# Attention scores computed already turned, with row maxima from a first rough product, and more of the elementwise work on GpSimd

## What is computed

```python
s = jnp.einsum('bqhd,bkhd->bhqk', qn, k_nope) + jnp.einsum('bqhd,bkd->bhqk', qr, k_rope)
pr = jax.nn.softmax(s.astype(jnp.float32) * scale, axis=-1).astype(v.dtype)
return jnp.einsum('bhqk,bkhd->bqhd', pr, v)
```

## Time and profile before

| | |
|---|---|
| median of 3 runs | 1148.6 us (1147.55 to 1149.5) |
| the profiled execution | 1144.88 us, its span 1143.1 us |
| granted PE clock | 0.996 of full over the span |
| busy, of the span | PE 98%, DVE 72%, ACT 49%, POOL 41% |
| attention, about 120 to 282 us | PE 97%, DVE 70%, ACT 73%, POOL 38% of it busy |

### The profile page before, as it was taken

One profiled execution on the slowest core, in us unless ns is written; L12 is line 12 of the kernel. 1 busy time (PEld: TensorE's weight loads), 2 busy tenths in 40 slices (PEclk: granted clock), 3 DMA queues, 4 the chain that ended last, 5 costly groups with the idle time before them and its releaser, 6 DMA issues.

```text
span 1143.1 us, 15837 instructions
## 1 busy us (share of the span) xinstructions
PE 1117.8 (98%) x5146; PEld 896.6 (78%) x5146; DVE 826.1 (72%) x1170; ACT 555.4 (49%) x986; POOL 464.2 (41%) x405
## 2 busy tenths in 40 slices
PE   8999999999999989999999999999999999999996
PEld 7787766665888867888888888888888888888885
DVE  7784976674468899878787878787876757757555
ACT  6312687775223454545454545454554545533332
POOL 0185642322566046765676567655310202211000
PEclk9999999999999999999999999999999999999999
DMA  6610000104652126444544454445896565533341
GB/s 209 222 44 26 1 12 13 38 19 164 204 202 104 56 81 205 165 138 152 178 165 138 154 176 165 138 155 172 330 344 204 190 197 192 168 108 118 92 143 74
DMA packets 138431, 161.60 MB, mean 141 GB/s; under 512 B 8755, under 2 KB 105354, under 8 KB 133770
## 3 DMA queue, kind: packets, MB, share of 16 engines
q1 hardware_dynamic: 138080, 160.82, 42.0%
q10 hardware_dynamic: 298, 0.11, 0.0%
HBM read 115.55 MB, written 45.35 MB: 141 GB/s over the span
## 4 chain that ended last, share of the span: by engine, by line
PE 86%; DVE 10%; issue 2%; ACT 1%; POOL 1%; DMA 0%; DVEq 0%; SPq 0%; POOLq 0%; ACTq 0%
PE ps L298 26%; PE ps L299 26%; PE ps L300 26%; PE ps L869 2%; PE ps L850 2%; DVE WL L2050 1%; PE ps L711 1%; PE ps L861 1%; DVE XL L1727 1%; DVE SF L2149 1%; DVE SF L2157 1%; DVE WDHL L1907 1%; DVE col L1918 1%; DVE XT L1721 0%; DVE R L1900 0%
## 5 line engine op out<-in xcount | busy, mean ns | idle before, releaser
L298 PE MATMUL ps<-XH,WH 128*128 128x512 f32 x722 | 287.1, 398 | 0.8 <-DVE WL L339 0.5
L300 PE MATMUL ps<-XH,WL 128*128 128x512 f32 x722 | 281.2, 390 | 0.0
L299 PE MATMUL ps<-XL,WH 128*128 128x512 f32 x722 | 281.1, 389 | 0.0
L298 PEld LDWEIGHTS ps<-XH,WH 128*128 128x128 f32 x722 | 135.6, 188 | 32.4 <-issue 3.0
L299 PEld LDWEIGHTS ps<-XL,WH 128*128 128x128 f32 x722 | 135.7, 188 | 29.1 <-issue 2.2
L300 PEld LDWEIGHTS ps<-XH,WL 128*128 128x128 f32 x722 | 135.5, 188 | 28.5
L298 PE MATMUL ps<-GHL,WH 128*128 128x512 f32 x394 | 153.6, 390 | 0.8 <-DVE WL L2050 0.7
L300 PE MATMUL ps<-GHL,WL 128*128 128x512 f32 x394 | 153.3, 389 | 0.0
L299 PE MATMUL ps<-GHL,WH 128*128 128x512 f32 x394 | 153.3, 389 | 0.0
L334 ACT ACTIVATE WH<-WR 128x1024 fp32r<-128x1024 f32 (+3 forms) x45 | 45.5, 1011 | 138.7 <-PE ps L300 129.4
L1476 ACT ACTIVATE SF<-ps,col 128x512 f32<-128x512 f32 x88 | 68.2, 778 | 74.6 <-PE ps L300 65.6
(11 more groups left out here) (241 smaller groups left out, 2250.8 us busy)
## 6 DMA issues: line engine op xcount, KB each, us to landing
TL<-in_w_up SPq DMA_DIRECT2D x48, 256.0 KB, 3.6
s_scratch<-XT SPq DMA_DIRECT2D x11, 1024.0 KB, 4.7
XT<-in_w_down SPq DMA_DIRECT2D x11, 1024.0 KB, 6.5
t_scratch<-XT SPq DMA_DIRECT2D x11, 1024.0 KB, 3.8
WR<-t_scratch SPq DMA_DIRECT2D x44, 256.0 KB, 2.7
TL<-s_scratch SPq DMA_DIRECT2D x44, 256.0 KB, 2.9
WR<-in_w_up SPq DMA_DIRECT2D x40, 256.0 KB, 3.5
WR<-in_w_down SPq DMA_DIRECT2D x33, 256.0 KB, 3.7
```

The lines of the kernel that those rows point to most:

```text
L298: pe.matmul(out, wh, xh, start=first, stop=False, skip_group_check=skip)
L299: pe.matmul(out, wh, xl, start=False, stop=False, skip_group_check=skip)
L300: return pe.matmul(out, wl, xh, start=False, stop=last, skip_group_check=skip)
```

## The change

The product of keys and queries is made with its sides exchanged, so that the scores come out with keys on the partitions, as `weigh` wants them. The row maximum then lies along the partition axis. It is found ahead, from a rough product: `rough(v)` multiplies only the high halves, 128 queries x 512 keys, in the old orientation; `maximum` reduces it as before into a column of `MXR`; `turn_max` turns four such columns with one small product against an identity; `max_rows` (DVE) writes them as four extra rows under the high half of the query (`QH[HEAD:MAXED]`). The high half of the key has four rows of ones there, so the exact product subtracts the maximum itself. `exponent` then needs no bias and writes straight into `PT`. There is no transpose and no copy.

The row sums lie along partitions now as well: `key_sum` (POOL) adds the four key tiles of a unit, three additions each, and `total` (PE, in place of the product with diagonals) sums over partitions with ones. `inverse` (DVE) turns the 128 x 512 result in 32 x 32 blocks and takes the reciprocals of one column of each block, `spread_rc` (ACT) spreads them, and `scale_rows` (DVE) turns them back and multiplies. `row_diagonals` and `row_scale` are gone. `q_low` of pairs 1 to 3 is on POOL, that of pair 0 stays on DVE. Rough tiles take two banks of PSUM in turn, exact ones two others. PE makes `rough(v + 3)` and `scores(v - 2)` in step v.

```diff
-            def scores(i, u):
...
-                ins = mm3(pe, s_bank(i * 16 + u)[:, :], QH[0:HEAD, s, h, tok], QL[0:HEAD, s, h, tok],
-                          KH[0:HEAD, s, h, :], KL[0:HEAD, s, h, :], True, True)
...
-                for k in range(TT):
-                    ins = pe.transpose(ps[4 + u % 2][:, k * P:(k + 1) * P], p_buf(i * 16 + u)[:, k * P:(k + 1) * P], ident[:, :])
+            def rough(v):
...
+                if v >= 2:
+                    pe.wait_ge(max_ready, v - 1)
+                pe.matmul(m_bank(v)[:, :], QH[0:HEAD, s, h, t * P:(t + 1) * P], KH[0:HEAD, s, h, :],
+                          start=True, stop=True).then_inc(m_ready, 1)
+
+            def turn_max(n):
+
+                pe.wait_ge(max_ready, 4 * n + 4)
...
+                pe.matmul(ps[1][0:TT, 0:P], MXR[:, n % 2, 0:TT], ident_r[:, :], start=True, stop=True).then_inc(max_turned, 1)
+
+            def scores(v):
...
+                if k == 0:
+                    pe.wait_ge(max_row, n + 1)
+                    pe.wait_ge(q_lo, n + 1)
+                    pe.wait_ge(k_lo, n + 1)
...
+                    pe.wait_ge(exp_done, v - 1)
...
+                pe.matmul(o, KH[0:MAXED, s, h, keys], QH[0:MAXED, s, h, :], start=True, stop=False)
+                pe.matmul(o, KH[0:HEAD, s, h, keys], QL[0:HEAD, s, h, :], start=False, stop=False)
+                pe.matmul(o, KL[0:HEAD, s, h, keys], QH[0:HEAD, s, h, :], start=False, stop=True).then_inc(s_ready, 1)
...
             def pair(i, last):
                 for u in range(4 * TT):
...
+                    v = 4 * TT * i + u
+                    if v + 3 < 2 * HEADS * TT:
+                        rough(v + 3)
+                    if v >= 2:
+                        scores(v - 2)
+                    if u % TT == 1:
+                        turn_max(v // TT)
...
+                act.activation(PT[:, (n + 2) % 4, k, :], s_bank(v)[:, :], ACT.Exp).then_inc(exp_done, 1)
+
+            def spread_rc(i, s):
...
+            def max_rows(n):
+                s, h = divmod(n % 4, 2)
+                dve.wait_ge(max_turned, n + 1)
...
+                dve.tensor_tensor(QH[HEAD:MAXED, s, h, :].rearrange("p (a q) -> p a q", a=TT),
...
             def inverse(i, s):
...
+                dve.transpose(RT, ps[7][:, :]).then_inc(rr_copied, 1)
...
             def scale_rows(i, s):
...
+                dve.transpose(RB[:, :], RT).then_inc(rc_ready, 1)
...
+            def q_low(n, summed):
...
+                pool.tensor_tensor(QL[0:HEAD, s, h, :], QF[0:HEAD, n % 2, :], QH[0:HEAD, s, h, :].bitcast(F32), ALU.subtract).then_inc(q_lo, 1)
...
+            def key_sum(n, k):
...
+                    pool.tensor_tensor(buf, buf, a[:, k, :], ALU.add).then_inc(sum_step, 1)
```

More of the change, by code:

```diff
@@ L105, in encoder @@
         ones = sb("ones", [P, P])
+        ident_r = sb("ident_r", [P, P], F32R)
+        MXR = sb("MXR", [P, 2, LINE // 2], F32R)
         WR = sb("WR", [P, 2, KT, P])
@@ L853, in weigh @@
             def weigh(i, s, ks):
                 if ks[0] == 0:
[L856 to L862, removed]
@@ L872, in weigh, with total @@
                     ins.then_inc(o_ready, 1)
+            def total(i, s):
+                pe.wait_ge(sum_step, 3 * (i * 4 + 2 * s + 2))
+                if i or s:
+                    pe.wait_ge(rr_copied, i * 2 + s)
+                pe.wait_ge(v_copied, i * 2 + s + 1 + (i < HEADS // 2 - 1) * (2 - s))
+                for h in range(2):
+                    ins = pe.matmul(ps[7][h * V_DIM:(h + 1) * V_DIM, :], ones[:, 0:V_DIM], SUM[2 * s + h], start=True, stop=True)
+                ins.then_inc(rr_ready, 1)
             def pair(i, last):
                 for u in range(4 * TT):
-                    turn(i, u)
-                    if u + 3 < 4 * TT:
-                        scores(i, u + 3)
-                    elif not last:
-                        scores(i + 1, u + 3 - 4 * TT)
+                    v = 4 * TT * i + u
[5 more added lines that the diff above has]
+                        turn_max(v // TT)
                     if i == 0:
@@ L939, in _ @@
             pe.wait_ge(acc_free, 16)
-            for u in range(3):
-                scores(0, u)
+            for v in range(3):
+                rough(v)
             for i in range(HEADS // 2):
@@ L954, in out_tile @@
                         weigh(HEADS // 2 - 1, 1, range(TT))
+                        total(HEADS // 2 - 1, 1)
                     if first and k == 3:
@@ L1348, in pair @@
                         if u == 3:
+                            q_split(0, 2)
+                            keep(1)
                             act.wait_ge(rot_done, 6)
@@ L1937, in pair @@
                 for u in range(4 * TT):
-                    if u + 2 < 4 * TT:
-                        maximum(i, u + 2)
-                    elif not last:
-                        maximum(i + 1, u + 2 - 4 * TT)
+                    v = 4 * TT * i + u
+                    if v + 2 < 2 * HEADS * TT:
+                        maximum(v + 2)
+                    if u % TT == 2:
+                        max_rows(v // TT)
                     if i:
                         if u == 0:
-                            q_low(i, 2)
-                        if u == 1:
+                            scale_rows(i - 1, 0)
+                        if u == 2:
                             k_low(i, 1)
-                        if u == 2:
+                        if u == 3:
                             output(i - 1, 0)
-                        if u == 7:
+                        if u == 6:
+                            inverse(i - 1, 1)
+                        if u == 8:
                             scale_rows(i - 1, 1)
@@ L2020, in _ @@
             rotate(0, 1)
-            maximum(0, 0)
+            maximum(0)
             add_turned(1)
-            maximum(0, 1)
+            maximum(1)
             for i in range(HEADS // 2):
```

344 lines of the change are left out of this document (182 added, 162 removed).

## The result

The changed kernel takes 1171.8 us (median of 4 runs, 1170.5 to 1174.9), the kernel before 1148.1 (4 runs, 1147.0 to 1149.5): ratio 1.021, 95% interval 1.0186 to 1.0233. It is slower by 23.7 us; 1146.4 was forecast, with a range up to 1153.

The account below looks back on a forecast made before the run. PE was taken to bound the attention from 151.19 to 281.88, DVE the first part of pair 0. Terms -6.4 + 1.2 + 7.1 - 4.1 = -2.2 us, from 1148.6 to 1146.4; range 1141.5 to 1153.

Parts of the forecast that it names:

- DVE in pair 0: Pair 0 up to step 8, where DVE is full: two `max_rows` come, one short reciprocal goes; +1.2 us.
- PE's saving behind it: PE from `values(1, 0)` on: rough tiles and turnings replace transposes, five more scores, a moved key projection; -6.4 us.
- the waits: PE's waits in the attention: +7.1 us of new ones, mostly for DVE, while the old 4.1 us are gone.
- The walk of steps: PE against DVE at listed prices, steps of pairs 0 to 3: waits of 1.2, 0.6, 1.5 and 2.8 us.
- ACT ... has two ops of slack per step. Nothing for it: ACT loses 64 copies and 64 accumulator reads, costs nothing; without slack each extra operation between exponentials would cost 0.3.
- the rule weighed: DVE instructions with two SBUF inputs and POOL's SBUF reads exclude each other; at worst the sum is near zero, not -2.2.
- What the rest of DVE's work costs: DVE beyond pair 0's start: 29.0 of 34.6 us per middle pair, but short margins give +7.1 us of new waits.
- The sign "a rough or small product dearer than its row": Listed sign of a wrong forecast: PE's rough tiles or small turnings costing more than the 0.23 and 0.11 us assumed.
- 0.22 plus half of 0.46: Chance of a faster kernel, given as 0.44: 0.22 for the rival of mostly absent waits (1142.3), 0.46 for the forecast.
- The prices that were never traced: Assumed prices in the attention: `max_rows` and 32 x 32 transposition on DVE 0.69 us each, POOL's addition 1.27.
- The rival of a slower DVE: DVE bounds the middle pairs at 35.8 us, with transpositions of 1.4 and POOL conflicts; +4.4 us, 1153.0, chance 0.24.
- the rival of POOL: POOL bounds the middle pairs, 40 us each at 2.15 per new operation; +10 us, 1158.6, chance 0.08.

Follow-up runs that it names:

- Experiments 1 to 4: Unused or moved tiles: kernel before with 576 bytes, 1161.4 us, other distances 1147.4 to 1162.6; changed kernel with new tiles last 1157.3, other placings 1171.1 and 1155.3.
- Experiment 7: Against kernel 2, ACT's query splits of pair 0 for units 2 and 3 moved earlier: 1155.4 us, 1.0053 to 1.0084.
- experiment 10: Against the kernel of Experiment 7, two query projections and `values(1, 0)` moved earlier on PE in pair 0: 1154.0 us, 1.0044 to 1.007.
- kernel 2: The changed kernel with both new tiles, `ident_r` and `MXR`, declared last, behind RB: 1157.3 us, 1.0057 to 1.0118.
- its twin: The changed kernel with `MXR` alone declared last and `ident_r` left ahead of WR: 1155.3 us, 1.0049 to 1.0088.
- kernel 12: Against the kernel of experiment 10, 30 products of 512 columns without use added at PE's idle places of pair 0: 1153.0 us, 1.0024 to 1.0052.
- experiment 5: Against kernel 2, 29 products of 512 columns without use added where PE idles in pair 0: 1156.5 us, 1.0049 to 1.0093.
- kernels 7 and 9: 7: the kernel of Experiment 7, 1155.4 us; 9: the same with 22 products without use on PE in pair 0, 1156.4 us, 1.0066 to 1.0095.
- experiments 10, 11: 11: the kernel of experiment 10 with DVE's last-pair weight splits moved from steps 5 and 6 to 9 and 12: 1154.8 us, 1.005 to 1.0076.

## Why the prediction was wrong

The time came out 25.4 us above the forecast of 1146.4. Three steps of the prediction failed, and by the numbers below they make 24.9 us: the layout, put at nothing (14.5); DVE in pair 0, put at +1.2 where it was +8.2 (7.0); and PE's saving behind it, put at -6.4 where it was about -3.5 (3.4 together with the waits).

**A term that was missing: +14.5 us.** The prediction has no term for where the two new tiles lie; it says only that two fills of constants "go into idle time of POOL". It prices instructions that the diff adds, removes and moves, and takes all other rows over unchanged. The two tiles change the address of every tile behind them, and 2166 products that the diff doesn't touch became 3% dearer. Experiments 1 to 4 show this from both sides. No rival covered it; the range ended at 1153.

The Trainium skill would have led the same way: TensorE: Matmul & The Clock Gate, "Step-by-step: what each phase is for", says that loading the next weights takes no SBUF read bandwidth from the running product, and SBUF — State Buffer, "Who interferes with whom", that PE waits on nobody. Neither leaves room for what the traces show: weight loads stayed at 188 ns, but the products went from 389 to 394 ns, and from 0.2268 to 0.2335 us apart, with the distance of streamed tile and weights alone. The measurement decides. That the two reads of PE meet is argued from which products changed, not shown; why the distance matters stays open.

**"DVE in pair 0 ... +1.2 us": measured +8.2.** `values(1, 0)` was forecast at 152.4; without the layout's part it came at 161.5, or 34.0 us after DVE's first low half of the keys, where it had been 25.8. Of these 8.2 us, 6.5 are idle time of DVE (7.3 us in that stretch, 0.8 before) and 1.7 are work. Two things failed.

- The step took DVE's stretch as a sum of its work ("there a shorter PE gives nothing and a longer DVE is paid for"). That holds while DVE stays full. The change makes a closed chain: `scores` wait for `max_rows`, the exponential for `scores`, the query split for the exponential, DVE's low half for the split. The walk of steps left out the first ten steps of pair 0, and "ACT ... has two ops of slack per step. Nothing for it" looked at ACT's load and not at what stands behind its wait. Experiment 7 takes 3.4 us off in the trace, experiment 10 another 2.2. The traces show this chain and its opening; in the time the gain is small (kernel 10 at 1.0057, kernel 2 and its twin at 1.0087 and 1.0069) and the intervals overlap, since a part of it is lost again behind `values(1, 0)`.
- The sum was short. By the order of the code DVE makes 12 maxima, not 11, ahead of what releases `values(1, 0)`, besides the two `max_rows`: +1.9 net of the reciprocal by the same rows. In kernels 10 and 12 `values(1, 0)` stands ahead of the twelfth, so that +1.2 would do. With the clock held (12) DVE idles as little as before (0.8 us) and `values(1, 0)` starts 28.0 us after the first low half of the keys: +2.2. The two `max_rows` are 1.4 of it and the reciprocal -0.2. Another 1.2 is in DVE's four low halves of the queries, 4.6 us together against 3.4 before; in kernel 12 and before they read:

```profile
L1952 DVE TENSOR_TENSOR GHL<-R,GHL x4: 681/1128/1779, 131.0 to 149.7; 96x512 fp32r<-96x512 f32 x4
```

```profile
L1913 DVE TENSOR_TENSOR GHL<-R,GHL x4: 678/725/1485, 126.7 to 144.4; 96x512 fp32r<-96x512 f32 x4
```

The longest, from 143.69 on, starts within 0.1 us of two POOL subtractions, 3.0 us together. That such meetings make it longer fits the rule weighed; it was not tested by itself.

**The low clock in pair 0** was not forecast: in the kernel after, it reads 0.66 to 0.83 there, where PE has gaps. Filler against it gained almost nothing while the chain stood (experiment 5) and about 2 us once the chain was opened (10 against 12). Executions of one and the same kernel say that the clock is not free even while the chain stands: of kernel 2, two at a mean granted clock of 0.988 and 0.989 took 1154.6 and 1155.4 us, two at 0.983 and 0.986 took 1159.2 and 1160.6; kernels 7 and 9 show the same. Only one execution of each was profiled, so where the others lost it isn't known, and the clock's price stays unsettled, at some 1 to 5 us.

**"What the rest of DVE's work costs", the middle pairs: nearly right.** Forecast were 35.5 to 36.5 us. Kernel 2 gives 36.8, in its windows of two middle pairs and of the last one:

```profile
182.36:219.16 36.80, 36.05 (x165) 22.67 (x166) 30.27 (x46) 17.40 (x33) 26.58 (x23) 1.00 0.04 10
219.16:255.95 36.79, 36.04 (x164) 22.66 (x166) 30.28 (x46) 17.40 (x33) 26.59 (x23) 1.00 0.10 29
255.95:292.14 36.19, 34.13 (x141) 17.78 (x141) 23.77 (x33) 16.37 (x28) 23.71 (x18) 1.00 0.34 117
```

DVE 30.3 (forecast 29.0), POOL 26.6 (25.9), and PE waits for `MXR` and `GHL`, as said. They gain 1.1 us each, not 1.9: their waits are about 1.3 us each, but PE's own work is 35.5, not the 34.6 of the forecast, for the reason below.

**"-6.4 us" of PE's work was too much; the waits were right in sum.** From `values(1, 0)` to the attention's end it takes 130.67 us in kernel 2 and 130.69 before; forecast was 3.4 less (-6.4 + 7.1 - 4.1). The list of waits names 4.8 us in that stretch, but it counts a wait only from the modelled end of the product before it. By the distances of starts, with the 0.1 us by which the product behind a wait comes late, PE waits 6.4 us in kernel 2 and 3.0 before: +3.4, where +7.1 - 4.1 = +3.0 was forecast. Both terms were too large, and their difference was nearly right. So PE's work fell by about 3.5 us, not by 6.4. PE in kernel 2 shows where the rest went:

```profile
184.16 0.50 PE L844 MATMUL ps<-WDHL,GHL 96*128 96x512 f32 x1
184.50 0.40 PE L870 MATMUL ps<-GHL,WDHL 100*128 100x512 f32 x1
...
185.19 0.39 PE L844 MATMUL ps<-WDHL,GHL 96*128 96x512 f32 x1
185.43 0.40 PE L870 MATMUL ps<-GHL,WDHL 100*128 100x512 f32 x1
...
191.45 0.22 PE L855 MATMUL ps<-ident_r,MXR 128*4 128x128 f32 x1
191.60 1.08 PE L896 MATMUL ps<-SF,ones 128*64 128x512 f32 x4
```

A rough tile costs the 0.23 us of its row where it follows scores or a projection (185.19), but 0.34 behind a `weigh` or a sum over partitions (184.16), and that is so for 19 of the 51 tiles of the stretch. Together they take 14.3 us, not 11.8. A small turning takes 0.15 us, not 0.11: 2.0 us, not 1.4. The sign "a rough or small product dearer than its row" had been named. The other terms hold: the transposes were 24.3 us (54 x 0.45; the 23.8 of the prediction is a slip), and the five scores more cost 3.8 in place of 3.5.

Two more slips of arithmetic are in the prediction, and neither decides anything: in the last pair the three terms named for PE add up to 7.6 us, not 6.7, and 0.22 plus half of 0.46 is 0.45.

**The prices that were never traced: right.** From the changed kernel, ns min/median/max:

```profile
L1946 DVE TENSOR_TENSOR GHL<-ps,ident x16: 682/684/685, 139.1 to 285.3; 4x512 fp32r<-4x512 f32 x16
```

```profile
L1953 DVE STREAM_TRANSPOSE SF<-ps x8: 716/717/717, 179.6 to 296.9; 128x512 f32<-128x512 f32 x8
```

```profile
L2516 POOL TENSOR_TENSOR GHL<-R,GHL x12: 1268/1278/1292, 169.5 to 274.1; 96x512 fp32r<-96x512 f32 x12
```

Forecast were 0.69, 0.69 and 1.27 us. The rival of a slower DVE needed 1.4 for the transposition and 35.8 us of DVE in a middle pair, which has 30.3: it falls. So does the rival of POOL, which is full in no middle pair (26.6 of 36.8 us). The measured time lies beyond both rivals' because of the layout, which neither has. POOL's neighbourhood may cost something, as the rule weighed has it: a low half of the output with both inputs in SBUF went from a median of 0.69 to

```profile
L1967 DVE TENSOR_TENSOR XL<-RB,XH x8: 691/1234/1471, 190.1 to 300.8; 128x512 fp32r<-128x512 f32 x8
```

## What to carry to other kernels

A new tile is an edit to every tile declared behind it. Declare it last, or look at the distance between what PE streams and its weights: here a distance changed by 64, 128, 576 or 640 bytes made 2166 products 3% slower, one changed by 512 did not, and one unused tile is a test of it. Where engines hand work to and fro in a fixed order, a sum of the busiest one's work is a lower bound only: walk the order, and ask of each operation on a third engine what it stands behind. And a product's price depends on what runs ahead of it: read it in each neighbourhood that the new order makes.

## What was not expected of the hardware

- Products of 512 fp32r columns start 0.2268 us apart or 0.233 to 0.2335, at the same granted clock, depending on the distance of streamed operand and weights: changed by 0 and by 512 bytes either way against changed by 64, 128, 576 and 640; weight loads take 188 ns in both.
- A rough tile, an fp32r product of 512 columns, took 0.23 us to the next start behind its like and 0.34 behind the fp32 products of `weigh` or of `total`.
- PE's granted clock, 1.00 throughout the attention before, read 0.57 to 0.88 over many stretches of 10 us of pair 0 in which PE idled 1 to 5.5 us, and 0.61 to 0.82 even in the full stretch behind them (experiments 10, 11). At the lower level products start 0.43 us apart.
